# Order of the first PE transposes and place of the pool-scale transpose in a one-core hybrid decoder layer

## The reference, cut to what matters

```python
def rmsnorm(x, g):
    xf = x.astype(F32)
    var = jnp.mean(xf * xf, axis=-1, keepdims=True)
    return (xf * lax.rsqrt(var + RMS_EPS) * g.astype(F32)).astype(x.dtype)

def project(x, ln_g, w_in):
    h = jnp.einsum('btd,dn->btn', rmsnorm(x, ln_g), w_in)
    ...
```

## Time and profile before

| | |
|---|---|
| three timed executions | 2063.23, 2060.35, 2063.58 us; median 2063.23 |
| the profiled execution, its own time | 2057.28 us |
| its span from first to last instruction | 2055.8 us |
| mean granted TensorE clock | 0.999 of full speed |
| PE busy, matmuls | 2039.5 us (99%) |
| DVE, ACT, POOL busy | 64%, 35%, 22% |
| mean DMA rate | 214 GB/s |

### The profile page before, as it was taken

One profiled execution on the slowest core, in us unless ns is written; L12 is line 12 of the kernel. 1 busy time (PEld: TensorE's weight loads), 2 busy tenths in 40 slices (PEclk: granted clock), 3 DMA queues, 4 the chain that ended last, 5 costly groups with the idle time before them and its releaser, 6 DMA issues. The chain is left out here.

```text
span 2055.8 us, 38380 instructions
## 1 busy us (share of the span) xinstructions
PE 2039.5 (99%) x13919; PEld 1944.5 (95%) x13919; DVE 1318.8 (64%) x1794; ACT 718.5 (35%) x885; POOL 457.2 (22%) x646
## 2 busy tenths in 40 slices
PE   9999999999999999999999999999999999999998
PEld 7888888899999999999999999999999999999997
DVE  5656666577777545567768676756465866655565
ACT  6433333332322333333333232333334433333333
POOL 1233322221211020045553112111112411111100
PEclk9999999999999999999999999999999999999999
DMA  8899999974555565566576567698888755555554
GB/s 233 259 317 325 309 325 301 283 204 139 174 145 156 168 190 173 158 195 195 167 231 182 169 189 223 196 304 263 284 264 285 247 165 168 167 164 170 153 162 149
DMA packets 348628, 439.60 MB, mean 214 GB/s; under 512 B 21484, under 2 KB 317356, under 8 KB 346248
## 3 DMA queue, kind: packets, MB, share of 16 engines
q1 hardware_dynamic: 293704, 291.75, 47.8%
q0 software_dynamic: 37264, 128.16, 18.9%
q10 hardware_dynamic: 17584, 18.70, 2.7%
HBM read 394.46 MB, written 48.22 MB: 215 GB/s over the span
## 5 line engine op out<-in xcount | busy, mean ns | idle before, releaser
L246 DVE TENSOR_TENSOR lo<-raw,hi 128x1024 fp32r<-128x1024 f32 x542 | 695.3, 1286 | 520.9 <-ACT hi L241 519.3
L270 PE MATMUL main<-XX,hi 128*128 128x320 f32 x3264 | 1028.4, 315 | 0.4 <-DVE XX L1708 0.2
L272 PE MATMUL main<-XX,lo 128*128 128x320 f32 x3264 | 1008.7, 309 | 0.0
L271 PE MATMUL main<-XX,hi 128*128 128x320 f32 x3264 | 1008.3, 309 | 0.0
L241 ACT ACTIVATE hi<-raw 128x1024 fp32r<-128x1024 f32 x542 | 569.8, 1057 | 879.2 <-PE main L272 539.9
L270 PEld LDWEIGHTS main<-XX,hi 128*128 128x128 f32 x3264 | 613.0, 188 | 10.2 <-issue 5.0
L271 PEld LDWEIGHTS main<-XX,hi 128*128 128x128 f32 x3264 | 613.1, 188 | 2.3
L272 PEld LDWEIGHTS main<-XX,lo 128*128 128x128 f32 x3264 | 612.7, 188 | 0.0
L257 PE MATMUL main<-XX,hi 128*128 128x512 f32 x1024 | 357.5, 393 | 1.8 <-DVE lo L246 1.8
L258 PE MATMUL main<-XX,lo 128*128 128x256 f32 x1024 | 286.9, 280 | 0.0
L257 PEld LDWEIGHTS main<-XX,hi 128*128 128x128 f32 x1024 | 191.7, 187 | 46.0 <-DVE lo L246 2.4
(11 more groups left out here) (301 smaller groups left out, 1512.8 us busy)
## 6 DMA issues: line engine op xcount, KB each, us to landing
raw<-w_in SPq DMA_DIRECT2D x416, 512.0 KB, 4.2
raw<-w_out SPq DMA_DIRECT2D x128, 512.0 KB, 3.6
kin<-cache_k POOLq DMA_DIRECT2D x64, 256.0 KB, 6.1
turnedK<-kout POOLq DMA_DIRECT2D x64, 256.0 KB, 5.4
deck<-turnedK POOLq DMA_DIRECT2D x8, 2048.0 KB, 9.0
projT<-stg ACTq DMA_DIRECT2D x35, 320.0 KB, 2.9
keep<-cache_v POOLq DMA_DIRECT2D x40, 256.0 KB, 3.5
deck<-cache_v POOLq DMA_DIRECT2D x24, 256.0 KB, 4.1
```

What stands on the lines that cost most here:

```text
L246: nc.vector.tensor_tensor(low, raw[:, slot, :, 0:width], high.bitcast(F32), ALU.subtract).then_inc(lo_ready, 1)
L270: nc.tensor.matmul(sums, wh, XH[:, k, :], start=first, stop=False)
L271: nc.tensor.matmul(sums, wh, XL[:, k, :], start=False, stop=False)
L272: mm = nc.tensor.matmul(sums, wl, XH[:, k, :], start=False, stop=last)
```

## The change

The two token transposes and the sample transpose of a channel block k now stand together, for each k. The wait ahead of the first transposes covers `ident` and `gN` alone; `pscN` counts on a semaphore of its own, and its transpose and copy move into `finish`, to j = 2 on PE (into bank 0 of `wide`) and j = 3 on DVE. The DMA issues and their order stay as they are. Two semaphores that were unused are renamed.

```diff
@@ on_sync
                 sp.dma_start(ident[:], t["c_ident"]).then_inc(s_small, 16)
                 sp.dma_start(gN[:], t["ln_g"][0].rearrange("(k p) -> k p", p=P)).then_inc(s_small, 16)
-                sp.dma_start(pscN[:], t["pool_scale"][0].rearrange("(k p) -> k p", p=P)).then_inc(s_small, 16)
+                sp.dma_start(pscN[:], t["pool_scale"][0].rearrange("(k p) -> k p", p=P)).then_inc(s_psc, 16)
@@ on_vector
                 nc.vector.tensor_copy(gT[:], bank[0][:, 0:KT]).then_inc(s_gcopy, 1)
-                nc.vector.tensor_copy(poolscT[:], bank[0][:, KT:KT + POOLW // P])
...
                 def finish(dve, q, j):
+                    if j == 3:
+                        dve.wait_ge(s_pscT, 1)
+                        nc.vector.tensor_copy(poolscT[:], sbank[0][:, 0:POOLW // P])
                     if j == 2:
@@ on_tensor
                 idle_products(WARM)
-                pe.wait_ge(s_small, 48)
-                nc.tensor.transpose(bank[0][:, 0:KT], gN[:], ident[0:KT, 0:KT])
-                nc.tensor.transpose(bank[0][:, KT:KT + POOLW // P], pscN[:],
-                                    ident[0:POOLW // P, 0:POOLW // P]).then_inc(s_gT, 1)
+                pe.wait_ge(s_small, 32)
+                nc.tensor.transpose(bank[0][:, 0:KT], gN[:], ident[0:KT, 0:KT]).then_inc(s_gT, 1)
 
                 def turn_tokens(c):
                     for k in range(KK * c, KK * c + KK):
...
                         for i, (c0, r) in enumerate(TT[0:2]):
                             nc.tensor.transpose(sbank[k % 4][:, c0:c0 + r], xN[i][0:r, k * P:k * P + P], ident[0:r, 0:r])
-                    for k in range(KK * c, KK * c + KK):
                         nc.tensor.transpose(sbank[k % 4][:, T_P:N], xN[2][0:N_S, k * P:k * P + P],
                                             ident[0:N_S, 0:N_S]).then_inc(s_xT, 1)
@@ finish(pe, q, j)
+                    if j == 2:
+                        pe.wait_ge(s_psc, 16)
+                        nc.tensor.transpose(sbank[0][:, 0:POOLW // P], pscN[:],
+                                            ident[0:POOLW // P, 0:POOLW // P]).then_inc(s_pscT, 1)
```

More of the change, by code:

```diff
@@ L403, in hybrid_layer @@
         s_diag, s_rb = sem("s_diag"), sem("s_rb")
-        s_kin, s_kinc, s_bvec, s_bvecc, s_outA, s_identb = (sem(n) for n in (
-            "s_kin", "s_kinc", "s_bvec", "s_bvecc", "s_outA", "s_identb"))
+        s_kin, s_kinc, s_bvec, s_bvecc, s_outA, s_psc = (sem(n) for n in (
+            "s_kin", "s_kinc", "s_bvec", "s_bvecc", "s_outA", "s_psc"))
         s_onehot, s_wi, s_zeros = sem("s_onehot"), sem("s_wi"), sem("s_zeros")
@@ L408, in hybrid_layer @@
         p_both, p_block = sem("p_both"), sem("p_block")
-        s_pairs, s_jn = sem("s_pairs"), sem("s_jn")
+        s_pscT, s_jn = sem("s_pscT"), sem("s_jn")
         (s_qz, s_wbc, p_scored, p_relu, p_sum, s_ipg, s_itr, s_iks, s_sc, s_prod, s_red,
```

## The result

Over 22 executions each the changed kernel takes 2066.97 us median (2061.76 to 2071.57) against 2061.89 before (2057.85 to 2067.01); the ratio is 1.0026, interval 1.0018 to 1.0035: slower, by 3.7 to 7.2 us. The profiled execution takes 2066.01 us, its span is 2064.4 us.

What follows compares the result with a forecast made beforehand. PE was taken to bound the kernel; 5.30 for row-count changes, -0.47 for the wait before the last chunk and +0.33 for pool scales gave +5.2 us. Forecast 2067.5 us, taken between 2066.3 and 2068.4; range 2062.0 to 2071.5.

Steps and rivals of the forecast that it cites:

- PE bounds the kernel behind the start; a loss there reaches the end: Whole kernel: PE busy 2039.5 of 2055.8 us; a microsecond lost in the first stage is one at the end.
- The early start gains nothing: Start: shorter first wait and moved pool scales save about 0.8 us, all ending at the 17.18 wait; gain 0.
- signs of being wrong: Groups behind 17.18 under 1.6 us, their start before 17.0, or new PE waits for ACT or DVE.
- Each change of row count costs 0.094 + 0.055 us: Token transposes: eight changes per group instead of two, 0.88 us more each, 5.3 us for six groups behind 17.18.
- The wait ahead of chunk 7 gives 0.47 us back: Before the last chunk's products, PE's wait for ACT was to vanish: -0.47 us.
- Pool scales +0.33 us: Next segment, j = 2: one 16-row transpose between two chunks costs +0.33 us, bounds 0.1 and 0.5.
- Landing of x part 2 unchanged: Start: POOL's issue at 6.92 and queue orders stay, so the 17.18 wait stays; upper bound 0.3 us later, taken 0.
- Sum: Whole kernel: +5.2 us; with the lower spacing +3.8, with late landing of x part 2 +5.7.
- the free order: Token transposes: six groups cost nothing more, only the pool scales' +0.3 remains, 2063.5 us; chance 0.12.
- the clock: At 17.18, behind PE's wait of about 2 us, the clock falls: +2.0 on top, 2069.5 us; chance 0.05.
- no other wait behind the start gave anything back: Place not named: an unknown wait gives back half of the loss, +2.5, 2064.9 us; chance 0.06.
- x part 2 came no sooner: Start: x part 2 lands earlier and 0.7 of the saved start survives, over a free order: -0.4; chance 0.02.

Runs made afterwards that it cites:

- experiment 1: Changed kernel without its turned transpose order (short first wait and moved pool scales stay); ratio to the kernel before 1.0005, interval 0.9993 to 1.0017.
- Experiments 3: Kernel before with blocks turned in pairs, so a group has four changes of row count; ratio to the kernel before 1.0015, interval 1.0004 to 1.0025.
- experiment 4: Changed kernel with sample transposes taking all 128 rows, the upper 64 zeroed once; ratio to the kernel before 1.0007, interval 0.9996 to 1.0017.
- experiment 2: Kernel before with the turned transpose order alone, wait and pool scales as before; ratio to the kernel before 1.0032, interval 1.0021 to 1.0043.
- experiments 9 to 11: Unchanged kernels profiled again: the kernel before a second and third time (2058.16 and 2060.95 us), the changed kernel a second time (2064.72 us).
- experiments 5: Kernel before, but POOL issues x part 2 without waiting for part 0; ratio to the kernel before 1.0005, interval 0.9992 to 1.0018.
- 6: Kernel before, but ACT issues x part 2 behind its own two parts; ratio to the kernel before 1.0013, interval 0.9999 to 1.0026.
- 7: Changed kernel with 128-row sample transposes, pool scales turned behind the products of chunk 0, x part 2 issued at once; ratio to the kernel before 1.0010.

## Why the prediction was right, step by step

- **PE bounds the kernel behind the start; a loss there reaches the end.** Right: the distance grows by 4.8 us, and the measured difference is 3.7 to 7.2.
- **The early start gains nothing.** Right within what the times can tell: experiment 1 gives a ratio of 1.0005, and the starts of the third group leave room for some 0.3 us. One step in it was wrong: PE was to stand about 2 us ahead of x part 2, and stood 1.24. The norm transpose came at 6.79 (7.1 was worked out; that it came sooner is luck, the zero products took 0.55 us less in this execution), but the first products came at 12.78, hardly sooner than 12.93. What held them I had not looked at: ACT's first weight split waited for the landing of weight chunk 0,

```profile
10.97 0.74 ACT L474 ACTIVATE hi<-raw 128x640 fp32r<-128x640 f32 x1 [1.08 <-DMA raw<-w_in]
```

  so the gain at the start was cut off once more ahead of the wait that I named. It lay in the same slack and changed nothing in the sum. But the prediction had called a new wait of PE for ACT or DVE, and a third group that starts before 17.0, signs of being wrong. The first came (0.57 us for DVE, line 492), the second in the changed kernel's second profile (16.93); both belong to the start, which was read less well than the rest.
- **Each change of row count costs 0.094 + 0.055 us.** Right: 0.88 us more per group by the periods (5.19 against 4.31), 0.88 was the value taken. The doubt was what stands behind a single sample transpose, 0.15 or 0.205; it is 0.20 in the rows. Experiments 3 and 4 show that it is the change and not the order, and the weight loader's waits show it directly: 6, 12 and 24 of 0.17 us behind 17 us with two, four and eight changes in a group, none in experiment 4. The rule of the Trainium skill that I set against it ("TensorE: Matmul & The Clock Gate", Part 3, The mechanism), by which the order would have been free, does not hold in this case: full rows behind full rows step by 0.11, and only a change of rows by 0.20. The same section also names a background weight buffer as a way for a load to run ahead, so it is the word "only" that the rows contradict.
- **The wait ahead of chunk 7 gives 0.47 us back.** Right: gone in the changed kernel and in experiment 2, back in 1; in 3 a part of it, about 0.2, is left.
- **Pool scales +0.33 us.** 0.35 in the rows.
- **Landing of x part 2 unchanged.** Right to some 0.3 us; start of the third group: 17.18, 17.32 and 17.73 in three profiles of before, 17.13 and 16.93 in two of the changed kernel, 16.7 to 17.4 in experiments 1 to 4.
- **Sum.** +5.2 worked out, +5.1 by the traces (4.79 + 0.35), and 5.1 us by the medians (2066.97 - 2061.89). That the forecast time, 2067.5, lies so near the median is in part luck: its base of 2062.3 was picked between one profiled and three timed executions, and the scatter is 9 us. Two of the side sums don't come out as written: the lower one is 3.7, not 3.8, and the one with late landing 5.5, not 5.7. The 8.6 us between the two first profiled spans are not the change alone: between 240 and 400 us the changed kernel's first profile runs 9 pairs of 0.352 us fewer of the same products, 3.2 us there alone, by the slower of the two paces of experiments 9 to 11. By one profile of each the price would have been overstated by two thirds. Compared at one pace, the end of that segment lies 418.90 - 413.84 = 5.1 us later (the slower), or 415.45 - 410.20 = 5.3 and 415.45 - 408.94 = 6.5 us (the faster).

Rivals: the free order is excluded by experiments 2 and 4; the clock did not fall in the changed kernel, whose granted clock stays at 1.00 through the stretch; no other wait behind the start gave anything back; x part 2 came no sooner than by some tenths.

## What to carry to other kernels

In a stream of short transposes (here float32, 64 rows among 128) each change of the weight load's row count cost 0.15 us, with the late start of what follows; so keep those of one row count together, or pad the odd one to full rows when PE is the bound. Giving the next engine its data sooner was worth nothing here, where PE is the limit: the first block of a group got ready for ACT about 0.7 us earlier, and ACT had 4 us to spare. And a saving ahead of a wait for a DMA is only a longer wait, as long as the DMA lands no sooner.

## What the runs showed of the hardware that I had not expected

- **Two paces of one matmul stream.** The pairs of lines 257 and 258 run at 160 / 463 = 0.346 us or at 160 / 454 = 0.352 us, for hundreds of pairs on end, at a granted clock of 1.00 and with PE without a gap in both. Six of the thirteen profiles hold the first (462 or 463 pairs between 240 and 400 us), seven the second (453 or 454). Over the 1024 pairs of the segment that is up to 7 us, and so a part of the 9 us by which executions of one kernel scatter. An execution may change its pace within the segment (the third profile of before: 142 pairs in 48.97 us between 100 and 150, 114 in 40 between 200 and 240); what sets it isn't known, and no run was made to find out.
- **Width is cheaper than a change.** With twelve transposes of 128 rows a chunk's period is 4.23 us, with eight of 128 and four of 64 in a row it is 4.31.
- **A clock that falls in a start full of short waits**: at gaps of 1.8 to 2.4 us in experiments 5 and 6, but not at 3.5 and 2.0 in 7. It cost 2.3 us in the one profile of 5, half the effect that the change itself had.
